# The last attention stage of a decoder trunk, reordered into pairs of units

## The reference, cut to what matters

```python
# selected branch: per query the keys of 8 chosen blocks of 64
scs = einsum(qb, kg) * scale - slopes * dist
p = softmax(where(dist >= 0, scs, NEG));  o_slc = einsum(p, vg)
# window branch: the last 512 keys
o_win = banded_attention(q, kw, vw, C_WINDOW, slopes)
return gates[..., 0:1] * o_cmp + gates[..., 1:2] * o_slc + gates[..., 2:3] * o_win
```

## Time and profile before

| what | value |
|---|---|
| device time, median of 3 | 773.97 us (770.73 to 774.15) |
| the profiled execution: its own time, its span | 772.57 us, 770.6 us |
| TensorE, matmul busy | 726.2 us (94% of the span) |
| TensorE, weight load busy | 625.1 us (81%) |
| VectorE busy | 543.6 us (71%) |
| ScalarE busy | 420.8 us (55%) |
| GpSimd busy | 189.7 us (25%) |
| exponentials, line 1783 | 128, 94.9 us |
| low parts, line 1855 | 192, 94.4 us |
| transposes, line 865 | 528, 81.8 us |
| high parts, line 1793 | 192, 81.0 us |
| first pass of the scores, line 1994 | 192, 74.4 us, mean 388 ns |

### The profile page before, as it was taken

The page is one execution under the profiler, slowest core; times in us unless marked ns, Lnnn a source line. Parts: engine busy times, 40 slices in busy tenths (PEclk is TensorE's granted clock), DMA queues, the critical chain, the costliest instruction groups (busy, mean ns, idle before and its releaser), DMA issues.

```text
span 770.6 us, 15601 instructions
## 1 busy us (share of the span) xinstructions
PE 726.2 (94%) x5980; PEld 625.1 (81%) x5980; DVE 543.6 (71%) x1263; ACT 420.8 (55%) x982; POOL 189.7 (25%) x118
## 2 busy tenths in 40 slices
PE   4999999999999999889999998989999999899996
PEld 4999878687777777668888886978999999788885
DVE  4796222044888888967779997998999999934232
ACT  5774122013566656657733333878999999722211
POOL 2674000000000000000143343416276552122120
PEclk9999999999999999999999999999999999999999
DMA  8620548165135621143154323300003101143331
GB/s 330 204 82 27 195 133 230 51 186 166 54 90 134 171 81 56 55 127 108 56 135 117 111 69 89 80 2 2 2 3 111 57 3 57 64 155 119 129 109 55
DMA packets 34090, 77.13 MB, mean 100 GB/s; under 512 B 5472, under 2 KB 14048, under 8 KB 33376
## 3 DMA queue, kind: packets, MB, share of 16 engines
q1 hardware_dynamic: 34016, 76.13, 32.6%
HBM read 57.77 MB, written 18.35 MB: 99 GB/s over the span
## 4 chain that ended last, share of the span: by engine, by line
PE 58%; DVE 15%; ACT 14%; issue 8%; DMA 4%; POOL 1%; SPq 1%; ACTq 0%; DVEq 0%; POOLq 0%
ACT n_probs L1783 5%; ACT n_probsT_high L1793 4%; DVE n_probs L1846 4%; PE o_acc L2224 3%; PE o_acc L2223 3%; PE o_acc L2222 3%; PE a_projected L199 3%; PE a_projected L201 3%; PE a_projected L200 3%; PE nat L823 3%; PE s_projected L199 3%; PE features L809 2%; PE s_projected L201 2%; PE s_projected L200 2%; PE n_turned L865 2%
## 5 line engine op out<-in xcount | busy, mean ns | idle before, releaser
L1783 ACT ACTIVATE n_probs<-n_probs,n_negated_max 128x640 f32<-128x640 f32 (+7 forms) x128 | 94.9, 741 | 18.3 <-DVE n_negated_max L1846 17.4
L1855 DVE SCALAR_TENSOR_TENSOR n_probsT_low<-n_turned,n_probsT_high 128x512 f16<-128x512 f32 (+3 forms) x192 | 94.4, 520 | 14.3 <-ACT n_probsT_high L1793 11.8
L183 POOL TENSOR_TENSOR w_and_keys_low<-w_raw,w_and_keys_high 128x1024 fp32r<-128x1024 f32 x6 | 15.0, 2503 | 290.6 <-ACT w_and_keys_high L168 290.4
L865 PE MATMUL n_turned<-identity,n_probs 128*128 128x128 f32 x528 | 81.8, 280 | 3.5 <-ACT n_probs L1783 2.8
L1793 ACT ACTIVATE n_probsT_high<-n_turned 128x512 f16<-128x512 f32 (+3 forms) x192 | 81.0, 457 | 4.6 <-PE n_turned L865 4.0
L1994 PE MATMUL n_scores<-w_and_keys_high,stacks 128*128 128x256 f32 (+2 forms) x192 | 74.4, 388 | 4.4 <-DVE n_negated_max L1846 4.3
L865 PEld LDWEIGHTS n_turned<-identity,n_probs 128*128 128x128 f32 x528 | 61.5, 143 | 12.4 <-ACT n_probs L1783 9.2
L1995 PE MATMUL n_scores<-w_and_keys_low,stacks 128*128 128x256 f32 (+2 forms) x192 | 61.6, 332 | 0.0
L199 PE MATMUL a_projected<-xT_high,w_and_keys_high 128*128 128x512 f32 x144 | 57.4, 398 | 0.9 <-ACT staged L208 0.7
L201 PE MATMUL a_projected<-xT_high,w_and_keys_low 128*128 128x512 f32 x144 | 56.4, 392 | 0.0
L200 PE MATMUL a_projected<-xT_low,w_and_keys_high 128*128 128x512 f32 x144 | 56.4, 391 | 0.0
(11 more groups left out here) (289 smaller groups left out, 2142.0 us busy)
## 6 DMA issues: line engine op xcount, KB each, us to landing
w_raw<-in_w_feat SPq DMA_DIRECT2D x23, 512.0 KB, 4.0
weights_then_b_and_s_raw<-features SPq DMA_DIRECT2D x30, 256.0 KB, 4.7
stacks<-a_parts SPq DMA_DIRECT2D x48, 128.0 KB, 3.9
features<-staged SPq DMA_DIRECT2D x22, 256.0 KB, 4.3
branches_b_c<-in_x SPq DMA_DIRECT2D x8, 512.0 KB, 4.3
silu_gates<-staged SPq DMA_DIRECT2D x16, 256.0 KB, 2.0
gatesT<-silu_gates SPq DMA_DIRECT2D x8, 512.0 KB, 5.5
keys_and_w_out_raw<-in_w_out SPq DMA_DIRECT2D x4, 1024.0 KB, 5.1
```

The source lines that it names most:

```text
L865: mm = nc.tensor.transpose(dst[:, j, :], src[:, c:c + P], ident[:, :])
L1783: nc.scalar.activation(pr[:, n % PS, 0:w], pr[:, n % PS, 0:w], ACT.Exp, scale=-1.0, bias=nmax[:, hb % 4, qt:qt + 1], accum_out=sums[:, hb ...
L1855: nc.vector.scalar_tensor_tensor(out=ptl[:, g % GS, 0:k, :], in0=tp[g % TS][:, 0:k, :], scalar=PSCALE, in1=pth[:, g % GS, 0:k, :], op0=ALU ...
```

## The change

The constant `TS` (slots for turned tiles, a PSUM bank each) goes from 3 to 4. The two output banks become one, so that the first values of a half wait for the copy of the half just before. TensorE's loop takes two units at a time: both scores, both turns, both values. VectorE takes both biases and then both low parts. ScalarE's loop is written by pairs too; its order of exponentials and high parts comes out as it was, but the copy of a finished half stands behind the second exponential of the next half's loop (unit n + 2) and ahead of the high part of its second unit.

```diff
@@ -1689,7 +1689,7 @@
         tiles.append(list(range(max(qt - 4, 0), qt + 1)) if n % HU < NT else list(range(qt + 1)))
     runs, before = softmax_chunks(tiles)
     AHEAD = 2
-    PS, TS, GS = 4, 3, 6
+    PS, TS, GS = 4, 4, 6
     GU = RC * HU
     SLABS = 3
     MASKED = [qt for qt in QT_ORDER if qt >= SEL_T]
@@ -1724,7 +1724,7 @@
         sums = sb("n_sums", [P, 4, NT], F32)
         sc = [ctx.enter_context(nc.psum_tensor(f"n_scores{i}", [P, (2 - i) * 512], F32)) for i in range(2)]
         tp = [ctx.enter_context(nc.psum_tensor(f"n_turned{i}", [P, 4, P], F32)) for i in range(TS)]
-        ov = [ctx.enter_context(nc.psum_tensor(f"n_outp{i}", [P, 512], F32)) for i in range(2)]
+        ov = ctx.enter_context(nc.psum_tensor("n_outp", [P, 512], F32))
 
         raw_in = [sem(f"n_raw_in{i}") for i in range(2)]
         consts_in, masked = sem("n_consts_in"), sem("n_bias_masked")
@@ -1800,15 +1800,17 @@
                         act.wait_ge(sig.stored[i], STORED)
                 if hb >= 2:
                     act.wait_ge(added, hb - 1)
-                nc.scalar.copy(red[:, hb % 2, :, :], ov[hb % 2][:, :].rearrange("p (q d) -> p q d", q=NT)).then_inc(headed, 1)
+                nc.scalar.copy(red[:, hb % 2, :, :], ov[:, :].rearrange("p (q d) -> p q d", q=NT)).then_inc(headed, 1)
 
             exponentials(0)
-            for n in range(UN):
-                if n + 1 < UN:
-                    exponentials(n + 1)
-                high_part(n)
-                if n % NT == 2 and n > NT:
-                    bring_out(n // NT - 1)
+            exponentials(1)
+            for wide in range(0, UN, 2):
+                for n in (wide, wide + 1):
+                    high_part(n)
+                    if n + AHEAD < UN:
+                        exponentials(n + AHEAD)
+                    if n == wide and n % NT == 0 and n > 0:
+                        bring_out(n // NT - 1)
 
         @block.vector
         def _(dve):
@@ -1868,7 +1870,7 @@
                 ch.link(nc.vector.tensor_tensor(s.unsqueeze(2), s.unsqueeze(2), gate_of(h, 2 - br), ALU.mult))
                 dve.wait_ge(added, LAST)
                 dve.wait_ge(valued, before[NT * (LAST + 1)])
-                ch.link(nc.vector.tensor_tensor(last, ov[LAST % 2][:, :].rearrange("p (q d) -> p q d", q=NT), over_blocks(s),
+                ch.link(nc.vector.tensor_tensor(last, ov[:, :].rearrange("p (q d) -> p q d", q=NT), over_blocks(s),
                                                 ALU.mult))
                 nc.vector.tensor_tensor(out, out, last, ALU.add).then_inc(headed, 1)
 
@@ -1878,16 +1880,19 @@
             ch.link(nc.vector.tensor_tensor(small[:, 1:2], small[:, 0:1], small[:, 0:1], ALU.mult))
             ch.link(nc.vector.tensor_scalar(small[:, 1:2], small[:, 1:2], 1.0 / HD, None, ALU.mult))
             ch.link(nc.vector.tensor_scalar(small[:, 2:3], small[:, 0:1], 0.5 * (1.0 - LAM_INIT), None, ALU.mult))
-            for n in range(UN):
-                if n + AHEAD < UN:
-                    add_bias(n + AHEAD)
-                low_part(n)
-                if n in SUMS_AT:
-                    a_sums(SUMS_AT.index(n))
-                if n == RSTD_AT:
-                    a_rstd()
-                if n % NT == 1 and n > NT:
-                    invert_sums(n // NT - 1)
+            for wide in range(0, UN, 2):
+                pair = (wide, wide + 1)
+                for n in pair:
+                    if n + AHEAD < UN:
+                        add_bias(n + AHEAD)
+                for n in pair:
+                    low_part(n)
+                    if n in SUMS_AT:
+                        a_sums(SUMS_AT.index(n))
+                    if n == RSTD_AT:
+                        a_rstd()
+                    if n % NT == 1 and n > NT:
+                        invert_sums(n // NT - 1)
             invert_sums(LAST)
             write_last()
 
@@ -2007,12 +2012,12 @@
                 h, br, qt = place(n)
                 hb = n // NT
                 g_of = h // RC
-                if n % NT == 0 and hb >= 2:
-                    pe.wait_ge(headed, hb - 1)
+                if n % NT == 0 and hb >= 1:
+                    pe.wait_ge(headed, hb)
                 for i, run in enumerate(runs[n]):
                     g = before[n] + i
                     pe.wait_ge(t_low, g + 1)
-                    values_run(nc, ov[hb % 2][:, HD * qt:HD * (qt + 1)], pth[:, g % GS], ptl[:, g % GS], run,
+                    values_run(nc, ov[:, HD * qt:HD * (qt + 1)], pth[:, g % GS], ptl[:, g % GS], run,
                                lambda kt: vbs[:, kt, KV + g_of, :, :] if br == 1 else vw[:, kt, g_of, :, :],
                                i == 0, i == len(runs[n]) - 1).then_inc(valued, 1)
 
@@ -2021,12 +2026,16 @@
             scores(1)
             pe.wait_ge(seam.s_summed, C_H)
             pe.wait_ge(sig.copied, sig.halves)
-            for n in range(UN):
-                if n + AHEAD < UN:
-                    scores(n + AHEAD)
-                turn(n)
-                if n >= 2:
-                    values(n - 2)
+            for wide in range(0, UN, 2):
+                pair = (wide, wide + 1)
+                for n in pair:
+                    if n + AHEAD < UN:
+                        scores(n + AHEAD)
+                for n in pair:
+                    turn(n)
+                for n in pair:
+                    if n >= 2:
+                        values(n - 2)
             values(UN - 2)
             values(UN - 1)
 
```

## The result

The changed kernel is slower: 775.53 us against 773.78, medians of 20 runs each, ratio 1.0038 (95% interval 1.0024 to 1.0052), which is 1.9 to 4.0 us. The profiled execution has a span of 773.4 us against 770.6. The forecast was 779.3, range 771.0 to 783.5: right in direction, almost twice too large.

The account below looks back on a forecast made before the run. The prediction took a ring of waits between ScalarE and VectorE to bound the kernel. Its terms, 5.4 - 2.8 + 2.8 - 0.1 = +5.3 us on the median of 773.97, gave 779.3, range 771.0 to 783.5.

Parts of the forecast that it names:

- the grouping is hidden: Rival: the delays of turns on TensorE fall into slack, so +2.5 us, 776.5; chance 0.22.
- the late turns: TensorE turns large units behind two units' scores, delaying ScalarE: 0.31 us seven times, 0.07 eight times.
- The ring: Last attention stage: ScalarE and VectorE hold each other up through high part, low part, bias, exponential; 23.15 us a head.
- TensorE's relief: Half of 128 changes from values to scores go, 5.1 us of TensorE time, counted as nothing because hidden.
- that rival: TensorE binds: its small waits pace the stage, so the 5.1 us come back, 768.6; chance 0.13.
- Term 1: ScalarE's copy now stands ahead of a high part that others wait for: net 0.36 us each, 15 copies, +5.4.
- Term 2: VectorE does the small unit's bias sooner, ending the four-tile exponential's wait: -0.40 us, seven times, -2.8.
- Term 3: TensorE by pairs: 5.1 us saved counts as nothing; later turns of large units cost +2.2 and +0.6 us.
- Costs put at nothing: Fourth slot frees nothing, though grouped turns need it; single output bank's copy is hidden with 1.4 us to spare.
- Term 4: Stage start +0.4 us (bounds 0 and 0.7); stretch after VectorE's long chain -0.5; -0.1 taken together.
- One sign I had named: ScalarE's total wait for VectorE down by more than 3 us would mean TensorE had paced the stage.

Follow-up runs that it names:

- after_split: Changed kernel, with TensorE turning each unit right behind its own scores, then both units' values; ratio 1.0007 to the kernel before.
- after_copy_late: Changed kernel, with ScalarE's copy back behind the high part of the third unit, single bank kept; 780.95 us, ratio 1.0107 to the kernel before.
- copy_early: Kernel before, with only ScalarE's copy of a finished half moved to where the changed kernel has it; 777.08 us, ratio 1.0055.
- dve_pairs: Kernel before, with only VectorE's order changed to both biases of a pair, then both low parts; 789.17 us, ratio 1.0205.
- one_bank: Kernel before, with the copy moved as in copy_early, a single output bank and four slots for turned tiles; 777.89 us, ratio 1.0053.
- pairs_copy_late: Kernel before, with TensorE's and VectorE's orders both in pairs; three slots, two banks and the copy's place kept; ratio 1.0016.

## Why the prediction came out as it did

The direction, the loop and the prices of three terms were right; the size was not. The prediction called anything within 0.5% no change, and the measured 0.38% lies there. By the number alone the rival "the grouping is hidden" (+2.5 us) comes closer to the measured 2.9 than the forecast's 5.3, but its mechanism failed: the late turns cost 0.44 a head in the trace, and taking them away gains 0.38.

- **The ring sets the pace: right.** The copy's place alone moves a head by 0.72. TensorE's relief, a mean of 362 ns for the first scores matmul in place of 388, buys nothing that shows: after_split gives it back (386 ns) and is faster. But TensorE stands in the loop too, by when its turns come: 0.76 us of waiting ahead of values cost 0.67 in after_copy_late. The rule of the Trainium skill (Perfetto Trace Analysis, Identifying the Most-Contended Engine) left that rival open; here the engines were too close for shares of busy time to decide; the chain of waits did, and copy_early bore it out. The rival's own sum, 768.6, takes 0.3 off for terms 2 and 4, which the prediction puts at 2.9 together; it doesn't say where the 0.3 comes from.
- **Term 1: right in mechanism and price.** 0.36 each forecast; 0.36 alone, 0.38 and 0.39 in the changed kernel.
- **Term 2: right for the changed kernel** (-0.46 for -0.40), but I gave it to VectorE's order. dve_pairs shows that VectorE's order alone costs 16 us. It takes both orders.
- **Term 3: right in size,** 0.35 and 0.09 for 0.31 and 0.07, and confirmed by after_split. The sign that went with TensorE's relief was worked out wrong: the mean was to fall by about 40 ns, it fell by 26, and the term's own 5.1 us over 192 matmuls make 27.
- **Costs put at nothing:** the bank, right, and only as long as the copy is early (one_bank against after_copy_late). The fourth slot was not priced: it is worth 0.34 a head, which the sum had silently, since it assumed turns that never wait for a slot.
- **What was mis-sized is how often the terms count.** I multiplied by eight heads. A head costs 0.56 (the terms gave 0.72 - 0.40 + 0.38 = 0.70; the rest, 0.14, I traced to no cause), and it does so from unit 34 to 126, 5.75 heads: 3.2 us. The first head has no copy in its first half, and in the second VectorE's chains pace the kernel, nearly whatever the copy does. 0.56 times six is 3.4, against 1.9 to 4.0 measured. Two heads of 0.70 that cost about nothing and 0.14 a head less in the others are 2.2 us of the 2.4 by which the forecast was too large.
- **Term 4** (-0.1) was +0.99 at the start, over its bound of 0.7, and some -1.6 behind it in these two profiles. Both go with the clock, and are probably chance. That they partly cancel in the spans is luck.
- One sign I had named was badly chosen: ScalarE's wait for VectorE fell by 4.1 us, which I had said would speak for TensorE. My own term 2 accounts for about 2.8 of it; where late turns delay a high part, moreover, the bias is in time. Waits for turned tiles rose to 9.8 us for the 8 forecast, and a head takes 23.72, as forecast.

## What to carry to other kernels

Where engines in a pipeline are all over 90% busy, find the loop of waits that closes on itself, and put side work such as an evacuation where the loop leaves that engine waiting; the same 0.46 us cost 0.36 more a few instructions earlier. Two engines that each follow a written order and feed each other are best regrouped together: here the one order alone cost 2.0%, the other alone 2.5%, and both together (pairs_copy_late) nothing that these runs can tell. Inside the group, do first what the other engine waits for: turning each unit right behind its scores gained 0.38 us a head. A resource that nobody waits for in the old order is not therefore free in the new one; recount it under the new order.

## What the runs showed of the hardware

Behind a run of values matmuls (16-bit operands) the first scores matmul takes some 0.08 us longer to the start of the next than behind another scores matmul: 0.31 for 0.23 us at 512 columns, 0.26 for 0.17 at 384, 0.20 for 0.12 at 256. Behind a run of transposes it is the same (after_split: 0.32, 0.26 and 0.20). And like idle stretches of TensorE were followed by a clock of 0.50 in one execution and of 1.00 in another. I estimate that as worth some 1 to 1.5 us, from the 1.16 to 1.69 us that the nine kernels gain in the second head; it is as much as half the effect studied: compare such kernels by the steady heads of a profile or by many runs, not by two spans.
